# Low parts of the weights one tile behind their high parts in four stages, and all of them on VectorE in the mixers

## The reference

```python
# first block, two layers i
h = swiglu(rms_norm(x, g[0]), w_gate, w_up, w_down);  x = x + 0.5 * rms_norm(h, g[1])
m = dilated_attention(rms_norm(x, g[2]), ...) if i == 0 else retention(rms_norm(x, g[2]), ...)
x = x + rms_norm(m, g[3])
h = swiglu(rms_norm(x, g[4]), ...);                    x = x + 0.5 * rms_norm(h, g[5])
# second block, two layers l ("mixer", then "mlp")
dq, dk, dv, c_q, c_kv_kr, xq, gate_logits = split(rmsnorm(x, g_mix) @ w_in)
y_diff = diff_attention(...) @ w_diff_o     # 8 heads, two causal softmax maps each, rotary q and k
y_mla  = latent_attention(...) @ w_mla_o    # 8 heads, low-rank q and kv, rotary parts
y_mem  = memory_cross_attention(...) @ w_cross_o   # 4 heads over 256 memory rows
x = x + (g0 * y_diff + g1 * y_mla + g2 * y_mem) @ w_out
x = x + square(relu(rmsnorm(x, g_mlp) @ w_mlp1)) @ w_mlp2
```

## Time and profile before

| | before |
|---|---|
| median of three runs | 2388.45 us |
| profiled execution, first to last instruction | 2387.5 us |
| TensorE matmul busy | 2351.7 us (98%) |
| TensorE weight load busy | 2020.1 us (85%) |
| VectorE busy | 1511.0 us (63%) |
| ScalarE busy | 1195.5 us (50%) |
| GpSimd busy | 283.9 us (12%) |
| granted TensorE clock | 0.999 of full speed |
| read from HBM | 408.31 MB, 171 GB/s |

### The profile page before, as it was taken

One profiled execution on the slowest core, in us unless ns is written; L12 is line 12 of the kernel. 1 busy time (PEld: TensorE's weight loads), 2 busy tenths in 40 slices (PEclk: granted clock), 3 DMA queues, 4 the chain that ended last, 5 costly groups with the idle time before them and its releaser, 6 DMA issues.

```text
span 2387.5 us, 34279 instructions
## 1 busy us (share of the span) xinstructions
PE 2351.7 (98%) x13900; PEld 2020.1 (85%) x13900; DVE 1511.0 (63%) x2307; ACT 1195.5 (50%) x1794; POOL 283.9 (12%) x247
## 2 busy tenths in 40 slices
PE   9999999999999999999999999999999999999999
PEld 8987778779979977777899887788998887888987
DVE  6555567776555658666665677756665687656654
ACT  4444454454444446444544565555554555554543
POOL 1100010000000000000001121434110122333000
PEclk9999999999999999999999999999999999999999
DMA  7755644466566656544666654445666554445554
GB/s 229 209 194 175 172 125 136 148 187 183 186 194 177 186 185 197 173 134 151 184 186 204 203 177 143 124 126 183 186 199 206 181 170 131 121 144 172 183 189 145
DMA packets 263278, 411.66 MB, mean 172 GB/s; under 512 B 13770, under 2 KB 129370, under 8 KB 263120
## 3 DMA queue, kind: packets, MB, share of 16 engines
q1 hardware_dynamic: 256256, 389.59, 53.2%
q0 software_dynamic: 6432, 19.28, 3.1%
q10 hardware_dynamic: 432, 0.59, 0.1%
HBM read 408.31 MB, written 1.10 MB: 171 GB/s over the span
## 4 chain that ended last, share of the span: by engine, by line
PE 85%; DVE 8%; ACT 4%; issue 1%; POOL 1%; DMA 0%; SPq 0%; ACTq 0%; DVEq 0%
PE banks L1926 16%; PE banks L1928 16%; PE banks L1927 16%; PE banks L1952 9%; PE banks L1961 9%; PE banks L1953 9%; DVE w_lo L2517 2%; ACT w_hi L2205 2%; PE banks L2015 1%; PE banks L2075 1%; PE banks L2028 1%; DVE probs L2712 1%; PE banks L1909 1%; PE banks L1910 1%; PE banks L1915 1%
## 5 line engine op out<-in xcount | busy, mean ns | idle before, releaser
L2517 DVE TENSOR_TENSOR w_lo<-w_raw,w_hi 128x1024 fp32r<-128x1024 f32 x688 | 838.9, 1225 | 618.1 <-ACT w_hi L2205 616.9
L2205 ACT ACTIVATE w_hi<-w_raw 128x1024 fp32r<-128x1024 f32 (+2 forms) x744 | 777.8, 1049 | 534.6 <-PE banks L1928 379.5
L1926 PE MATMUL banks<-w_hi,xt_hi 128*128 128x512 f32 (+2 forms) x1056 | 432.3, 409 | 7.0 <-DVE xt_lo L2545 3.6
L1952 PE MATMUL banks<-xt_hi,w_hi 128*128 128x256 f32 x1728 | 426.5, 283 | 4.7 <-DVE w_lo L2517 3.1
L1953 PE MATMUL banks<-xt_hi,w_lo 128*128 128x256 f32 x1728 | 425.2, 283 | 0.0
L1928 PE MATMUL banks<-w_hi,xt_lo 128*128 128x512 f32 (+2 forms) x1056 | 413.3, 391 | 0.0
L1927 PE MATMUL banks<-w_lo,xt_hi 128*128 128x512 f32 (+2 forms) x1056 | 412.4, 391 | 0.0
L1952 PEld LDWEIGHTS banks<-xt_hi,w_hi 128*128 128x128 f32 x1728 | 326.6, 189 | 6.6 <-DVE w_lo L2517 3.4
L1953 PEld LDWEIGHTS banks<-xt_hi,w_lo 128*128 128x128 f32 x1728 | 326.7, 189 | 0.0
L1926 PEld LDWEIGHTS banks<-w_hi,xt_hi 128*128 128x128 f32 x1056 | 198.9, 188 | 52.3 <-DVE w_lo L2517 9.0
L1961 PE MATMUL banks<-xt_lo,w_hi 128*128 128x256 f32 x1728 | 243.0, 282 | 0.0
(11 more groups left out here) (438 smaller groups left out, 3042.4 us busy)
## 6 DMA issues: line engine op xcount, KB each, us to landing
w_raw<-in_w_mlp SPq DMA_DIRECT2D x128, 512.0 KB, 3.7
w_raw<-in_w_in SPq DMA_DIRECT2D x104, 512.0 KB, 3.7
w_raw<-in_ffn_w_gate SPq DMA_DIRECT2D x88, 512.0 KB, 3.9
w_raw<-in_ffn_w_up SPq DMA_DIRECT2D x88, 512.0 KB, 4.2
w_raw<-in_ffn_w_down SPq DMA_DIRECT2D x88, 512.0 KB, 3.6
w_raw<-in_attn_w_in SPq DMA_DIRECT2D x72, 512.0 KB, 3.8
w_raw<-in_ret_w_in SPq DMA_DIRECT2D x64, 512.0 KB, 3.8
w_raw<-in_ret_w_out SPq DMA_DIRECT2D x16, 512.0 KB, 3.8
```

Of the source, the lines that this page charges most:

```text
L1926: pe.matmul(bank, xh, wh, start=(c == 0), stop=False)
L1952: pe.matmul(out[f], hi[:, cols], xh, start=(c == 0), stop=False)
L2205: act.activation(k.w_hi[i % SPLIT][:, 0:m], k.raw[i % RAW][:, 0:m], ACT.Copy).then_inc(*ev.mark(k.w_hi_made, ("w_hi", i)))
L2517: dve.tensor_tensor(lo, raw, hi.bitcast(F32), ALU.subtract).then_inc(*ev.mark(k.w_lo_made, ("w_lo", i)))
```

## The change

The step `split` becomes two steps, `high` and `low`. `split(i)` puts `high` of tile i in the list, then the low parts that are still due, and notes the low part of tile i as due. Where `low_later` is false that low part follows at once, and the order is the one of before. Where it is true it follows after the `high` of the next tile, and so after everything that the list holds between the two splits. `low_later` is set in the dilated stage from its start, in retention after the first two blocks of columns, and in the mixers after the memory's tiles. It is false in the ffn and mlp stages. `self.share = 2` goes, so in the mixers VectorE makes all low parts. SyncE's loads hang on the `low` step.

```diff
@@ -453,6 +453,7 @@
 
         self.tiles, self.blocks, self.uid = [], 0, 0
         self.hold_at, self.held = None, []
+        self.low_due, self.low_later = [], False
         self.share, self.act_share, self.flip = 0, 2, 0
         self.gain_plan, self.gain_at = self.gains_in_order(), 0
         self.x_event = [[("x", 0, h, c) for c in range(2)] for h in range(HALVES)]
@@ -540,10 +541,20 @@
         return self.gain_at - 1
 
     def split(self, i):
-        self.step("split", i, "pool" if self.share and i % self.share == 0 else "dve")
+        self.step("high", i)
+        self.low_parts()
+        self.low_due.append((i, "pool" if self.share and i % self.share == 0 else "dve"))
+        if not self.low_later:
+            self.low_parts()
+
+    def low_parts(self):
+        for i, by in self.low_due:
+            self.step("low", i, by)
+        self.low_due = []
 
     def tile_used(self, i):
         if i == self.hold_at or self.held:
+            self.low_parts()
             self.held.append(i + SPLIT)
         else:
             self.split(i + SPLIT)
@@ -712,6 +724,7 @@
         for n, (kind, i, j) in enumerate(self.stages):
             self.st = n
             self.act_share = 3 if kind == "mix" else 2
+            self.low_later = False
             self.share = 0
             self.following = self.stages[n + 1] if n + 1 < len(self.stages) else None
             dict(ffn=self.ffn, mlp=self.mlp, dilated=self.dilated, retention=self.retention, mix=self.mix)[kind](i, j)
@@ -719,7 +732,7 @@
             for half in range(HALVES):
                 self.pending(half, c)
                 self.step("store", half, c, self.x_event[half][c])
-        self.plan = [s for s in self.plan if s[0] not in ("split", "load") or s[1] < len(self.tiles)]
+        self.plan = [s for s in self.plan if s[0] not in ("high", "low", "load") or s[1] < len(self.tiles)]
         self.plan = [s for s in self.plan if s[0] != "next_gain" or s[1] < len(self.gain_plan)]
 
 
@@ -1118,6 +1131,7 @@
     def dilated(self, i, j):
         a = self.a
         self.feed(order="classes")
+        self.low_later = True
         self.step("masks_seen")
         q, k = self.put("da_q", 0, [P, HALVES, D]), self.put("da_k", 8, [P, HALVES, D])
         pairs = [(self.put(f"da_qt{n}", at, [P, DC, SEQ]), self.put(f"da_kt{n}", at + 8, [P, DC, SEQ])) for n, at in enumerate((16, 72))]
@@ -1786,7 +1802,6 @@
 
         def outputs():
             yield from need("qt", "kt", "v")
-            self.share = 2
             yield from attend("diff", 2, diff_done)
             yield from need("cqt")
             yield from attend("cross", 2, divided("cross", o_cross, CROSS_D, 2, 2 * DIFF_H + MLA_H))
@@ -1849,7 +1864,7 @@
             if i >= RAW:
                 q.wait_ge(*(yield from ev.of("w_lo", i - RAW)))
             sp.dma_start(dst, t.view).then_inc(*ev.mark(k.w_landed[i % RAW], ("w_raw", i), by=16))
-        if what == "split":
+        if what == "low":
             i = of[0] + RAW
             if i < len(k.tiles):
                 t = k.tiles[i]
@@ -2196,7 +2211,7 @@
                 cols = slice(c * BLOCK, (c + 1) * BLOCK)
                 act.dma_start(k.gain_tile[0][:, cols], k.gain_plan[0][cols].partition_broadcast(P)).then_inc(*ev.mark(sem, (name, 0), by=16))
 
-        if what == "split":
+        if what == "high":
             i = of[0]
             m = k.tiles[i].nk * k.tiles[i].n
             q.wait_ge(*(yield from ev.of("w_raw", i)))
@@ -2509,7 +2524,7 @@
             dve.memset(k.probs.free[0][0][:, :], 0.0).then_inc(*ev.mark(k.dve_done, ("fill_ready",)))
             dve.memset(k.minus_half[:, :], -0.5).then_inc(*ev.mark(k.dve_done, ("minus_half",)))
 
-        if what == "split" and of[1] == "dve":
+        if what == "low" and of[1] == "dve":
             i = of[0]
             m = k.tiles[i].nk * k.tiles[i].n
             q.wait_ge(*(yield from ev.of("w_hi", i)))
@@ -3232,7 +3247,7 @@
             pool.dma_start(k.causal[:, :], a["c_causal"]).then_inc(*ev.mark(k.masks_landed, ("masks",), by=16))
             q.wait_ge(*(yield from ev.of("minus_half")))
 
-        if what == "split" and of[1] == "pool":
+        if what == "low" and of[1] == "pool":
             i = of[0]
             m = k.tiles[i].nk * k.tiles[i].n
             q.wait_ge(*(yield from ev.of("w_hi", i)))
```

## The result

The changed kernel takes 2399.24 us (median of 4 runs, 2398.63 to 2399.94) against 2388.68 us before (4 runs, 2387.96 to 2388.94): ratio 1.0044, 95% interval 1.003 to 1.0058. It is 10.6 us slower, the forecast was 7.1. The profiled span went from 2387.5 to 2397.3, by 9.8 us. In all lines after, the change has moved the code down by 15.

A forecast was written before the change was run, and what follows sets the result against it. TensorE's matmul stream, busy 98%, was taken as the bound, with 35.8 us idle to win. Losses of 14.6 us less gains of 7.5 gave 7.1 us slower: 2388.45 + 7.1 = 2395.5 us, range 2386 to 2403.

The forecast's parts named there:

- Long steps: Low parts late behind long VectorE steps: losses 5.7 us per mixer, 2.6 retention, 0.6 dilated last group, sum 14.6.
- the keys: Mixer, rotation of the keys: low parts behind both rotations make TensorE late, loss 1.8 us in each mixer.
- the first tiles: Mixer, first tiles after the memory's: low part behind two normalizing steps that wait for GpSimd's powers, loss 2.0 us each.
- Retention: Retention, rotation of the queries: two tiles get their low parts late behind the rotations, loss 2.6 us.
- a held power: Added low parts can hold up GpSimd's powers, 0.4 us more per mixer at the keys' rotation; left out of the sum.
- The rule named in the prediction: VectorE with two SBUF inputs contends with a GpSimd instruction reading SBUF; the later one is blocked for the whole instruction.
- the other stretched row: Mixer attention: two scalings that take 0.3 us alone took 2.18 us at 1492.91 beside GpSimd's low part.
- Gains, dilated and retention: Stalls behind a parked VectorE go: 2.1 us gained in the dilated stage, 1.4 us at the retention heads.
- The two stalls that I counted: Dilated stage: TensorE stalls of 0.92 us at 322.41 and 1.18 us at 446.59, forecast to go, gain 2.1 us.
- The heads' ring: Retention heads, chain from statistics to next statistics: turns in 3.7 us in place of 5.5, gain 1.4 us.
- Attention: Mixer attention: row maxima come before a low part and VectorE's load is even; gain 2 us per mixer, from 0 to 5.
- VectorE's waits: Sign that the prediction is right: VectorE's wait for ScalarE's high parts falls from 617 us by 300 or more.

The follow-up runs named there:

- parts 2 and 6: part 2, and part 6: kernel before with only 21 low parts behind long steps one tile late, 2417.52 us; with the changed kernel's order, 2404.85 us.
- part 3: Changed kernel with low parts ahead of long steps, without GpSimd's share, and low parts right behind high parts again from each mixer's last product on: 2378.38 us.
- Part 1: Changed kernel with GpSimd's share kept, 2398.01 us; kernel before with only the share taken away, 2401.45 us.
- part 4: The run of part 3 with low parts one tile late also in ffn and mlp stages, between feed and last product: 2376.47 us.
- part 2: Changed kernel with due low parts put ahead of rotations, bank normalizations and the last octets' softmax: 2379.81 us; the same with GpSimd's share, 2380.65 us.
- part 7: Kernel before with only two low parts late: retention's query rotation, 2391.61 us; or the one ahead of the query rotation in each mixer, 2391.04 us.

## Why the prediction was right

The mechanism held. The late places are those that it named, with stalls of 1.3 to 2.1 us on the low part, and parts 2 and 6 of the experiments show that nothing else makes most of the loss: it goes with these steps and comes back with them. Point by point:

- **Long steps.** Mixers: 5.7 us forecast each, 5.7 and 7.5 measured. The first is exact in sum (1.5 + 2.0 + 2.2), but by luck: the keys are 0.4 us over and the first tiles 0.5 under. The keys' rotation was taken to start 0.9 us earlier and starts 0.55 earlier (1442.92 before, 1445.87 now, where all runs 3.51 us later). The first tiles cost less since the memory's normalizations now start 0.5 us earlier, the first at 1378.29 (the point on powers says why). The second mixer repeats the first but for 1.5 us of half clock and 0.3 at its first tiles. Retention: 2.6 forecast, 2.3 and 1.5 of half clock measured.
- **The missing term: the clock.** The prediction priced a stall at its idle time. At two of its places TensorE was granted half of its clock (1.2 in place of 2.4 GHz) for some 3 us after 1.8 us of idle time: seven matmuls 0.43 us apart in place of 0.234. This is 3.0 us of the 9.8.
- **The missing term: the stage's end.** "It is false in the ffn and mlp stages" was taken for "nothing changes there". The mixer's flag still holds while its last tiles are released, and the share had covered that. This is 2.2 us (part 3).
- **The missing term: a power held up.** The dilated stage's first tiles lost 0.9 us. GpSimd's second power takes 0.55 us before. After, VectorE's low part starts 0.17 us ahead of it:

```profile
221.97 1.46 POOL L3236 TENSOR_TENSOR row_scale<-stat,minus_half 128x1 f32<-128x1 f32 x1 [1.01 <-DVE stat L2520]
```
```profile
221.80 1.22 DVE L2532 TENSOR_TENSOR w_lo<-w_raw,w_hi 128x1024 fp32r<-128x1024 f32 x1
```
```profile
223.57 0.45 PE L2104 MATMUL banks<-row_scale,ident 128*32 128x1 f32 x16 [1.20 <-POOL row_scale L3236]
```

  TensorE waits 1.20 us for it, 0.30 before. In the mixers the two powers of the queries went from 6.13 to 7.10 us in the same way and nobody waited for them. At the key rotation, where the prediction had looked for it, the powers took 3.33 us as before. So the 0.4 us that the prediction would have added there for a held power is not what makes the keys 0.4 us over. The rule named in the prediction (the Trainium skill, SBUF — State Buffer, "Who interferes with whom") agrees with the two that were held. I left it out of the sum since no row of before showed a power held. That reading was wrong: the 2.54 us in the earlier trace rows are a power of 1.02 us and one of 1.56, and a low part of VectorE starts at 1377.78, 0.37 us ahead of the second. In the changed kernel no low part stands there and the second takes 1.01:

```profile
1377.78 1.05 DVE L2517 TENSOR_TENSOR w_lo<-w_raw,w_hi 128x864 fp32r<-128x864 f32 x1
...
1378.15 1.56 POOL L3221 TENSOR_TENSOR stat<-stat,minus_half 128x4 f32<-128x4 f32 x1
```
```profile
1378.16 1.01 POOL L3236 TENSOR_TENSOR stat<-stat,minus_half 128x4 f32<-128x4 f32 x1
```

  So the later order freed one power in each mixer (the 0.5 us of the first tiles) and held up others.
- **A reading that was too narrow.** "Has two operands in SBUF" fits the product sum L3209, but not the other stretched row: the scaling at 1492.91 reads one tensor, `norm_sums`, and took 2.11 us; GpSimd's low part ran from 1492.62 to 1494.99. No number of the sum hangs on it.
- **Gains, dilated and retention.** 2.1 forecast, 3.9 measured. The two stalls that I counted gave 1.1 and 1.25 us, one at 451.6 that I hadn't counted gave 1.05, and three smaller steps the rest (-0.3, -0.45, +0.3). The heads' ring turns in 3.57 us (statistics at 1109.81 and 1113.38), forecast 3.7, and gave 1.7 us for 1.4.
- **Attention.** 2.0 each forecast, 2.9 and 2.8 measured. VectorE's load did not grow, as forecast: 30.9 us busy in 36.7 with four low parts more. The stall at 1489.28 is gone, though another grew from 0.62 us (at 1494.07) to 1.58 (at 1498.88). But I treated order and share as two small terms. Part 1 shows that the lost share alone costs 7 us, that the order alone gains 1.6, and that together they gain 2.9. That the total came near was luck: the split behind it was wrong.
- **VectorE's waits** fell by 196 us where 300 or more was forecast: 421 us are left, 359 of them in the ffn and mlp stages, where VectorE has little else to do (part 4); in the three kinds of stages that changed, 61 are left. The load in the mixers is 73% (247.3 of 338.9), as forecast, and L3209 takes 0.69 us on average, 1.21 before.

The three missing terms make 3.0 + 2.2 + 0.9 = 6.1 us, the gains were 3.8 us larger than forecast, and the long steps without the clock 0.3: 7.1 + 6.1 - 3.8 + 0.3 = 9.7. So the forecast's nearness in sum is in part luck: errors of 6.4 and 3.8 us with opposite signs.

## What to carry over

Before an operation is moved one tile later in a queue in order, list what the queue holds between the two places: the few long steps there (21 of 744) cost 16 us, and nearly everywhere else the same move gained. Put the late operation ahead of these steps and keep it late elsewhere: 9.0 us faster than before (part 2), where the plain edit was 10.6 slower, and 12.5 with the ends of the mixers and the ffn stages set right as well (parts 3 and 4). And look at how flags end at a stage's edge, not only at where they are set.

## What the runs showed of the hardware

- The same stall may or may not bring TensorE's clock down. After 1.8 us of idle time at retention's query rotation it fell to half for 3 us in the profiled executions of the changed kernel and of the runs with the share kept and with 21 late parts, and it stayed at full in that of the run with two late parts. At the last octet, with the same steps in the same order, it fell after 2.10 us of idle time and stayed at full after 2.09 (part 7). So the length of the stall alone does not decide. What does is open. A fall costs 1.2 to 1.6 us on top of the stall.
- A low part on GpSimd (2.4 us) takes from VectorE nearly what it saves there: with nine low parts (10.9 us) moved to GpSimd in a window, VectorE was busy 1.3 us less. An instruction of 0.69 us beside them averaged 1.97 us.
- It works in the other direction as well: a power of 0.55 us took 1.46 us when VectorE's low part began 0.17 us ahead of it.
- The first 240 us differ from run to run by up to 2 us by themselves, while later places repeat to 0.05 us between two runs of the same order, but for stretches at half clock (1.4 us at the last octet). For edits of 1 us the place is a better measure than the total.
